# A two-layer decoder trunk on one core: query groups between the first attention scores, and the last weight rows of two projections taken chunk by chunk

## The reference

```
z = rmsnorm(x) @ w_in                        # 1024 -> four groups of heads
y_a = B * causal_conv3(C * h')               # short gated convolution
y_b = swish(layernorm(causal_conv31(GLU)))   # conformer convolution
y_c = moba_attention(q, k, v)                # 4 heads of 64, partial rotary, blocks of 256
y_d = mla_attention(cq, ckv, kr)             # 4 heads: q = rmsnorm(cq) @ w_uq, k/v = rmsnorm(ckv) @ w_ukv
x = x + rmsnorm(concat(y_a..y_d) @ w_out)
f = (silu(g) * v) @ w_ffn_down, with g, v = causal_conv3(rmsnorm(x) @ w_ffn_up)   # width 2816
x = x + rmsnorm(f)
```

## Time and profile before

| | |
|---|---|
| median of 3 runs | 1242.11 us |
| profiled execution | 1241.49 us |
| its span | 1239.7 us |
| TensorE products busy | 1201.6 us, 97% |
| weight loads busy | 1010.7 us, 82% |
| VectorE, ScalarE, GpSimd busy | 822.6, 582.3, 208.9 us |
| granted TensorE clock, mean | 0.998 |
| chain that ended last | TensorE 87%, VectorE 5%, GpSimd 4% |

### The profile page before, as it was taken

The page is one execution under the profiler, slowest core; times in us unless marked ns, Lnnn a source line. Parts: engine busy times, 40 slices in busy tenths (PEclk is TensorE's granted clock), DMA queues, the critical chain, the costliest instruction groups (busy, mean ns, idle before and its releaser), DMA issues.

```text
span 1239.7 us, 15562 instructions
## 1 busy us (share of the span) xinstructions
PE 1201.6 (97%) x6044; PEld 1010.7 (82%) x6044; DVE 822.6 (66%) x1160; ACT 582.3 (47%) x879; POOL 208.9 (17%) x190
## 2 busy tenths in 40 slices
PE   6999998999999999999999999999999999999996
PEld 6888877888888888888898887787988888888885
DVE  4699667568666666544759977757766666664453
ACT  4455466545444444434545735746444444444432
POOL 1285155110000000000006822612000000000000
PEclk9999999999999999999999999999999999999999
DMA  8232322534333333456633333135233323326563
GB/s 244 81 86 83 89 44 99 168 109 119 99 89 102 96 92 102 160 196 207 201 94 90 85 89 93 68 120 170 69 102 102 101 87 101 102 87 204 178 226 121
DMA packets 157083, 147.36 MB, mean 119 GB/s; under 512 B 6831, under 2 KB 137811, under 8 KB 157011
## 3 DMA queue, kind: packets, MB, share of 16 engines
q1 hardware_dynamic: 156432, 145.64, 38.4%
q10 hardware_dynamic: 579, 0.74, 0.2%
HBM read 140.07 MB, written 2.10 MB: 115 GB/s over the span
## 4 chain that ended last, share of the span: by engine, by line
PE 87%; DVE 5%; POOL 4%; issue 2%; ACT 1%; DMA 1%; POOLq 0%; DVEq 0%; ACTq 0%
PE ps L508 28%; PE ps L510 27%; PE ps L509 27%; POOL cf_out L840 2%; PE ps L733 1%; PE ps L758 1%; POOL rms_r L831 1%; POOL prob L857 1%; PE ps L570 1%; POOL wsp L415 1%; DVE yt L911 1%; DVE xn L931 1%; DMA rows<-in_vectors 1%; DVE wsp L415 1%; PE ps L621 0%
## 5 line engine op out<-in xcount | busy, mean ns | idle before, releaser
L508 PE MATMUL ps<-xn,wsp 128*128 128x512 f32 (+2 forms) x1136 | 419.0, 369 | 12.3 <-DVE xn L931 12.3
L510 PE MATMUL ps<-xn,wsp 128*128 128x512 f32 (+2 forms) x1136 | 416.2, 366 | 0.0
L509 PE MATMUL ps<-xn,wsp 128*128 128x512 f32 (+2 forms) x1136 | 416.1, 366 | 0.0
L415 DVE TENSOR_TENSOR wsp<-raw,wsp 128x1024 fp32r<-128x1024 f32 (+1 forms) x250 | 311.3, 1247 | 156.9 <-ACT wsp L407 156.6
L407 ACT ACTIVATE wsp<-raw 128x1024 fp32r<-128x1024 f32 (+1 forms) x256 | 266.8, 1043 | 164.2 <-PE ps L510 132.3
L508 PEld LDWEIGHTS ps<-xn,wsp 128*128 128x128 f32 (+1 forms) x1136 | 215.2, 189 | 49.2 <-DVE xn L931 14.5
L510 PEld LDWEIGHTS ps<-xn,wsp 128*128 128x128 f32 (+1 forms) x1136 | 215.1, 189 | 35.2
L509 PEld LDWEIGHTS ps<-xn,wsp 128*128 128x128 f32 (+1 forms) x1136 | 215.3, 189 | 34.8 <-issue 0.5
L508 PE MATMUL ps<-wsp,hid 128*128 128x512 f32 (+1 forms) x488 | 189.7, 389 | 0.0
L510 PE MATMUL ps<-wsp,hid 128*128 128x512 f32 (+1 forms) x488 | 189.1, 387 | 0.0
L509 PE MATMUL ps<-wsp,hid 128*128 128x512 f32 (+1 forms) x488 | 189.0, 387 | 0.0
(11 more groups left out here) (147 smaller groups left out, 1301.7 us busy)
## 6 DMA issues: line engine op xcount, KB each, us to landing
raw<-in_w_ffn_up SPq DMA_DIRECT2D x88, 512.0 KB, 3.8
raw<-in_w_ffn_down SPq DMA_DIRECT2D x88, 512.0 KB, 4.2
raw<-in_w_in SPq DMA_DIRECT2D x40, 512.0 KB, 3.8
raw<-in_w_out SPq DMA_DIRECT2D x32, 512.0 KB, 3.5
x<-in_x SPq DMA_DIRECT2D x4, 512.0 KB, 8.1
xn<-xn SPq DMA_DIRECT2D x8, 256.0 KB, 3.2
out_x<-x SPq DMA_DIRECT2D x4, 512.0 KB, 4.0
xn<-kr SPq DMA_DIRECT2D x8, 128.0 KB, 3.1
```

Source lines behind the costliest of these rows:

```text
L415: eng.tensor_tensor(wsp[:, u % SPLIT, 1, 0:nk * n], raw[:, (l * NU + u) % RAW, 0:nk * n], fp(wsp[:, u % SPLIT, 0, 0:nk * n]), ALU.subtract ...
L508: pe.matmul(dst, a[0], b[0], start=start, stop=False, skip_group_check=True)
L509: pe.matmul(dst, a[0], b[1], start=False, stop=False, skip_group_check=True)
L510: return pe.matmul(dst, a[1], b[0], start=False, stop=stop, skip_group_check=True)
```

## The change

There are two parts.

**Attention.** The three query groups are no longer made before the steps. TensorE makes G_MR right behind scores(0), the first G_MQ behind scores(1) and the second behind scores(2). The unread products stay only at steps 4 to 15, one each; their bank 4 now holds the second G_MQ first, so the one of step 4 waits until VectorE has taken that group. VectorE takes the rotary group at step 0 and the remainders of the two G_MQ at steps 2 and 3, at the end of what it does there. ScalarE copies them at steps 1 and 2. GpSimd's three rotary passes come behind probability tiles 0, 1 and 3.

**Last rows.** For chunks 2 and 3, the last three weight rows of both projections are done first for chunk 2 and then for chunk 3. A row's weights are released by chunk 3. In the output projection the transposes of chunk 1 stand between the two. The sum of squares, the variance and the update of chunk 2 move ahead, into the loop over the last rows; in the output projection the x^T of chunk 1 does too.

```diff
+LAST_ROWS = 3
-LATENT_BANKS = (5, 3, 6, 7, 0, 1, 2)
+LATENT_BANKS = (5, 3, 6, 7, 0, 1, 4)
 TensorE:
+            def last_rows(l, u0, nk, stage):
+                for c in (2, 3):
+                    if stage == MIX and c == 3:
+                        transposes_x(2 * l + 1, MIX, 1)
+                    for k in range(nk - LAST_ROWS, nk):
+                        if c == 2:
+                            weights_ready(l, u0 + k)
+                        last = chunk_product(u0 + k, k, nk, stage, c)
+                        if k == nk - 1:
+                            last.then_inc(y_done, 1)
+                        elif c == 3:
+                            last.then_inc(row_done, 1)
+                def queries(i):
+                    if i == 0:
+                        pe.wait_ge(lat_ready, l * 4 + 4)
+                    u, g = (U_UR, G_MR) if i == 0 else (U_UQ, G_MQ + i - 1)
+                    weights_ready(l, u)
                     bank_taken_over(l, g)
+                    dense(u, bank_of(g), [pair(hid[:, CQN + j]) for j in range(3)], c0=max(i - 1, 0) * P)\
+                        .then_inc(group_done, 1)
-                        bank_free(l, (G_MQ + 1, G_MK + 1)[t])
+                        bank_free(l, (G_MK - 1, G_MK + 1)[t])
                     if t < N_ATT:
                         scores(t)
-                    for _ in range(2 if t < TRAIL else 1 if t < N_ATT // 2 else 0):
+                    if t < 3:
+                        queries(t)
+                    elif TRAIL < t < N_ATT // 2:
+                        if t == 4:
+                            bank_free(l, G_MQ + 1)
                         keep_clock()
 GpSimd:
+                    if t == 0:
+                        pool.wait_ge(q_taken, l + 1)
+                        pool.tensor_tensor(ml_shuf[:, :], ml_shuf[:, :], rope_d[:, 1, :], ALU.mult).then_inc(rot_sin, 1)
+                    if t == 1:
+                        pool.wait_ge(rot_sin, l + 1)
+                        pool.tensor_tensor(ml_rot[:, :], ml_rot[:, :], ml_shuf[:, :], ALU.add).then_inc(rot_done, 1)
-                    if t == 2:
+                    if t == 3:
                         pool.wait_ge(rot_hi, l * 5 + 5)
 VectorE, attention steps, behind the mask, the reciprocal and the remainder of the transposed probabilities:
+                    if t == 0:
+                        group_ready(G_MR, l)
+                        dve.tensor_tensor(ml_rot[:, :], ps[:, bank_of(G_MR), :], rope_d[:, 0, :], ALU.mult)
+                        dve.stream_shuffle(ml_shuf[:, :], ps[:, bank_of(G_MR), :], [(j + 16) % 32 for j in range(32)])\
+                           .then_inc(q_taken, 1)
+                    if t in (2, 3):
+                        i = t - 2
+                        dve.wait_ge(qn_hi, l * 2 + i + 1)
+                        dve.tensor_tensor(ml_q[2 * i][:, 1, :], ps[:, bank_of(G_MQ + i), :], fp(ml_q[2 * i][:, 0, :]),
+                                          ALU.subtract).then_inc(qn_ready, 1)
 VectorE, output projection, second half:
+                    if n == KD - LAST_ROWS + 1:
+                        token_var(rms_no(l, MIX, "y", 2))
+                        normed_lo(l, MIX, 1)
                     split_lo(dve, l, U_OUT + KD + n + LEAD)
+                    if n == KD - LAST_ROWS + 1:
+                        update(l, MIX, 2)
-                    if n == 7:
-                        normed_lo(l, MIX, 1)
-                token_var(rms_no(l, MIX, "y", 2))
-                update(l, MIX, 2)
                 token_var(rms_no(l, MIX, "y", 3))
 ScalarE, output projection, second half:
+                    if n == KD - LAST_ROWS + 1:
+                        square_y(l, MIX, 2)
+                        normed_hi(l, MIX, 1)
                     split_hi(act, l, U_OUT + KD + n + LEAD)
```

More of the change, by code:

```diff
@@ L586, in first_groups, with chunk_product @@
                             transposes_x(n, stage, j)
+            def chunk_product(u, k, nk, stage, c):
+                w = weights(u)
+                t = slice(c * P, (c + 1) * P)
+                for f in range(2):
+                    last = product(ps[:, y_bank(stage, c) + f, :], (hid[:, k, 0, t], hid[:, k, 1, t]),
+                                   (w[:, 0, 0, f * HALF:(f + 1) * HALF], w[:, 1, 0, f * HALF:(f + 1) * HALF]),
+                                   k == 0, k == nk - 1)
+                return last
             def row_product(l, u, k, nk, stage, half):
                 weights_ready(l, u)
-                w = weights(u)
                 for c in (2 * half, 2 * half + 1):
[L593 to L597, removed]
+                    last = chunk_product(u, k, nk, stage, c)
                     if k == nk - 1:
@@ L782, in _ @@
                             pe.wait_ge(pt_ready, (l + 1) * N_ATT)
-                        row_product(l, U_OUT + half * KD + k, k, KD, MIX, half)
-                        if half == 1 and k in (4, 6):
-                            transposes_x(2 * l + 1, MIX, (k - 4) // 2)
+                        if half == 0 or k < KD - LAST_ROWS:
+                            row_product(l, U_OUT + half * KD + k, k, KD, MIX, half)
+                        elif k == KD - LAST_ROWS:
+                            last_rows(l, U_OUT + KD, KD, MIX)
+                        if half == 1 and k == 4:
+                            transposes_x(2 * l + 1, MIX, 0)
                 first_groups(l, 2 * l + 1, MIX, U_UP, G_UP)
@@ L798, in _ @@
                             bank_free(l, G_UP + 2 * NF - 1)
-                        row_product(l, U_DOWN + half * NF + k, k, NF, FFN, half)
+                        if half == 0 or k < NF - LAST_ROWS:
+                            row_product(l, U_DOWN + half * NF + k, k, NF, FFN, half)
+                        elif k == NF - LAST_ROWS:
+                            last_rows(l, U_DOWN + NF, NF, FFN)
                         if half == 1 and l + 1 < DEPTH and k in (13, 16):
@@ L1248, in _ @@
                 for n in range(NF):
+                    if n == NF - LAST_ROWS + 1:
+                        token_var(rms_no(l, FFN, "y", 2))
                     split_lo(dve, l, U_DOWN + NF + n + LEAD)
+                    if n == NF - LAST_ROWS + 1:
+                        update(l, FFN, 2)
                     if n == 0:
@@ L1269, in _ @@
                         normed_lo(l, FFN, 1)
-                token_var(rms_no(l, FFN, "y", 2))
-                update(l, FFN, 2)
                 token_var(rms_no(l, FFN, "y", 3))
@@ L1445, in _ @@
                                    ACT.Copy).then_inc(vl_hi, 1)
-                for i in range(2):
-                    group_ready(G_MQ + i, l)
-                    act.activation(ml_q[2 * i][:, 0, :], ps[:, bank_of(G_MQ + i), :], ACT.Copy).then_inc(qn_hi, 1)
                 for t in range(N_ATT + ATT_TAIL):
@@ L1531, in _ @@
                 for n in range(NF):
+                    if n == NF - LAST_ROWS + 1:
+                        square_y(l, FFN, 2)
                     split_hi(act, l, U_DOWN + NF + n + LEAD)
@@ L1543, in _ @@
                         normed_hi(l, FFN, 1)
-                square_y(l, FFN, 2)
                 square_y(l, FFN, 3)
```

32 lines of the change are left out of this document (6 added, 26 removed).

## The result

The changed kernel is slower. The median of four runs is 1274.17 us (1272.79 to 1275.53), beside 1242.2 us for the kernel before (1242.01 to 1242.38): a ratio of 1.026, with an interval from 1.0247 to 1.0273. The profiled execution took 1275.53 us, with a span of 1273.7 us and a mean granted clock of 0.966; before it was 1241.49, 1239.7 and 0.998.

The account below looks back on a forecast made before the run. TensorE, busy nearly all the span, was taken to bound the kernel. Terms +2.32 - 0.98 - 1.85 + 0.14 - 1.92 = -2.29 us gave 1239.2 profiled, 1239.8 median; range 1237.4 to 1242.7.

Parts of the forecast that it names:

- The last rows: Both projections' last rows: -0.98 and -1.85 us at output projection to FFN, +0.14 at down projection, -1.92 at the end.
- the first FFN group at once: Output projection to FFN, layer 0: first groups follow the last row without a stand, at 257.75 instead of 258.94.
- transposes behind VectorE's normed x: FFN, layer 0: chunk 2's transposes wait 0.2 us for VectorE, starting at 266.70 instead of 267.68, gain 0.98 us.
- the last update without one in front: End of layer 1: chunk 3's variance at 1231.33 instead of 1233.25 behind update(2), gain 1.92 us.
- The wait for row 7: Output projection: row 7 is needed before VectorE has its remainder, costing 0.36 us with the signal.
- The stand at the start: Attention opening: TensorE waits 1.85 us at scores(0) until VectorE's subtraction frees the first key group's bank.
- The wait at step 4: Attention: the unread product waits for VectorE's subtraction of the last query group, going on 1.32 us late at 162.29.
- rival A: Attention: the wait at step 4 is hidden, 1.32 us less per layer, time 1237.2 us; 15%.
- The attention term: Attention opening: removed products, added switches and waits net +1.16 us per layer, 2.32 for two.
- Rival B: After the output projection: VectorE's chain to normed(2) is longer, both hand-overs give nothing, 1242.6 us; 15%.
- the two hand-overs: Output projection to first FFN groups: gain 0.98 us in layer 0 and 1.85 us in layer 1.
- rival C: Attention opening: new stands and removed products halve the clock, +18.8 us over two layers, 1258.6 us; 5%.

Follow-up runs that it names:

- the experiment with the start filled: Changed kernel plus eight unread products ahead of scores(0), wait at step 4 kept: 1247.88, 1254.71, 1254.77 and 1271.19 us.
- the experiment with few unread products: Kernel before with only the last-rows part of the change, minus the seven unread products of steps 0 to 3 per layer: 1267.01 us.
- the stand at step 4: Kernel before with only the last-rows part, plus a wait for VectorE's reciprocal before step 4's unread product: 1240.54, 1253.39, 1257.81, seven from 1269.02 to 1272.06 us.
- the three runs at 1248: Changed kernel with each query group ahead of its step's scores: nine of twelve runs 1232.53 to 1235.17 us, three at 1248.52 to 1248.7.

## Why the prediction was wrong

**What held.** The prediction's own terms came out within 0.15 us each. The last rows gave -4.5 us for a forecast of -4.61: the first FFN group at once, transposes behind VectorE's normed x (0.06 us, the chain that was taken to bind), and the last update without one in front. The wait for row 7 is there: 269.38 to 269.97 is one spacing of 0.227 and 0.36 more, as worked out. The stand at the start was 1.77 us for a forecast of 1.85 (1.93 by the starts, 151.07 where 149.14 was due), with the releaser that was named. The wait at step 4 was there too, so rival A fell. Its product was forecast for 162.29 and came at 163.85, of which up to 1.7 us is the low stretch of 3.4 us ahead of it (its products at twice the time): without that it would have come at about 162.2. The attention term as a whole is borne out where the clock did not fall: in layer 0 of the experiment with the start filled, whose unread products are as long as the stand that they cover, attention took 66.22 us, 1.06 more than before, for a forecast of 1.16. Rival B fell with the two hand-overs.

**The step that failed is the dismissal of rival C.** The prediction said: "If the granted clock fell from the level of 2.4 GHz to that of 1.2, the 9.39 us of the opening would take twice as long, +18.8 us over two layers: 1258.6", and gave it 5%. It failed twice.

*The chance.* Two observations spoke against it, and both were of other work. The stretch from 181 to 210 at 1.00 without unread products is the second half of attention, whose scores use 96 rows where those of the first half use 64, and whose products are packed closer (190 in 29 us, for 96 in the 16 us before it): after the change the level came back soon after that half began (step 16 at 198.8, the clock at 203.0). The stand of 2.28 us lies between long projections. The prediction also says that no row of the trace shows a fall, and that is wrong: in the kernel before the clock falls at 1233.8, 3.7 us after TensorE's last product is done. The question was what holds the level in the steps 0 to 15, and there the kernel before offered only that it stays at 1.00 with 19 unread products and without a stand. Steps 0 to 3 without their seven products lose the level behind a stand of 0.73 us (the experiment with few unread products). A 1.68 us stand with them in place loses nothing. Removing fillers and adding stands were costed as separate terms; the clock took them together.

*The size.* I let the low level end with the opening. It has two parts: a short stretch behind the start (3.4 and 6.8 us), and a long one of 37.5 us in each layer behind the step-4 stand. Once low, steps 4 to 15 of this kernel stay low with unread products that go with 1.00 in the kernel before (elsewhere the level came back within these steps, after 3.4 and 20.5 us). So the price was not one opening of 9.39 us but the rest of the first half of attention. In numbers: attention grew by 18.53 + 20.00 = 38.5 us; 2.3 of it is the forecast of its instructions and waits, and 36.2 is left for 85.3 us at the low level, 0.42 us for each; the two layers with the start filled give 0.44 (9.0 for 20.5). All of the 85.3 at twice the time would cost 42.7; part of the rest lies at the changes between kinds of products, where the spacing less than doubles: from an unread product to the first transpose it is 0.59 us at the low level (171.66 to 172.25) and 0.34 at the full one (163.85 to 164.19).

**Where the loss comes from is shown by taking it away.** Without the wait at step 4: 1239.25. With the start filled as well: 1235.59. The last rows with the attention of before: 1235.79. With the unread products doubled: 1252.03, stands unchanged. So the loss comes through the clock, from stands in thin steps (steps that give TensorE few and short products), and not from the waits' own 2.8 us a layer. The Trainium skill (TensorE: Matmul & The Clock Gate, Part 1) says that the low level is the default and that activity lifts it. The rows agree as far as they go: 0.43 us spacing behind the stand for the 426.7 ns that the Trainium skill gives there. What Part 4 of the same page of the Trainium skill says, that transposes do not count as work in the same way, is neither borne out nor refuted here: steps 4 to 15 at the low level consist of scores, transposes and one unread product, and the level returned in steps that also have transposes.

**Not settled.** Why executions of one kernel differ (1240.54 to 1272.06 for the stand at step 4; layer 0 and layer 1 within one execution with the start filled), and how much filling a step needs before the level is safe. That the second query block at full occupancy lifted the clock between the two stands of the changed kernel is read from the windows, not tested by itself. The 0.43 us stand at step 5 is the likely cause of the three runs at 1248; with it filled five runs show none, which three of twelve before it doesn't prove.

## What to carry to other kernels

A product that nobody reads, in a step that is thin for TensorE, is not waste until a run without it shows the clock still at its upper level; taking out seven a layer (4.6 us over two layers) cost 31 us here. Where an edit removes fillers (unread products) and adds a wait in the same stretch, price the clock first, over the whole stretch up to the next dense work, and not by stands that the kernel survives elsewhere. The row of the granted clock is to be read ahead of the busy shares, which stayed at 97%. Moving the query groups ahead of the scores instead of behind, so that dense work covers VectorE, and filling step 5 turned the whole change from +32 us into -9, of which the last rows alone give 6.

## What the runs showed of the hardware

The granted clock depends on what went before. Steps 4 to 15 run at 1.00 throughout in the kernel before, and once the clock had fallen in or ahead of them they were at 0.50 for 37.5 or 41.0 us in both layers of three profiles (the change, its attention alone, few unread products), for 20.5, 6.8 and 3.4 us in others. A stand of 1.0 us of TensorE at step 4 came before most of these falls, and one of 0.73 us in steps without fillers, while 1.68 us ahead of dense products did nothing in ten runs. The fall comes after the stand, not in it: the stand ends at 163.85, and the clock falls at 165.5; over all profiles it came 0.2 to 2.2 us behind the end of the stand. In 4 of the 12 experiments the runs of one kernel spread by 10 us or more, so a single profile of a kernel near this edge says little: the one profile of the stand at step 4 shows the mildest of its ten runs.
